# GpSimd makes the low part of every fourth weight chunk in the expert passes

## The chip, the cores and the metric

One core of a Trainium2 chip runs the whole kernel. The metric is the device time of one launch in microseconds. Three runs of the kernel before took 2875.26, 2880.69 and 2881.18 us; their median is 2880.69.

## The reference, cut to what matters

The reference is two transformer blocks over 512 tokens of width 1024 in float32. The part that the change touches is the `peer` layer of the first block: each token picks 16 of 16384 experts for each of 8 heads by product keys, and each expert is one row of `expert_u` and one of `expert_v`:

```python
cand = (s_top[:, :, 0, :, None] + s_top[:, :, 1, None, :]).reshape(T, PEER_HEADS, K * K)
...
# act = gelu(h . u_e) of the chosen experts, weighted by the softmax of the scores,
# output = sum over the chosen experts of weight * act * v_e
```

The kernel computes it in two ways. For 128 of the tokens it gathers the rows of the chosen experts. For the other 384 it multiplies with all experts, and masks out those that were not chosen.

## The kernel before

Matrix products are made exact to about float32 by splitting both operands into a high part (`wH`, rounded to fp32r) and a low part (`wL`, the rest), and adding three products: `three` (L380) issues low activations times high weights, high activations times low weights, and high times high.

Weights come in chunks of 128 x 2048 float32, 1 MB each, numbered through the whole kernel. Chunk k is loaded by the SP queue into `stage[k % 2]` (`load`, L330), ScalarE copies it to `wH[k % 4]` (`split_hi`, L342, line L347 in the profile), VectorE subtracts to get `wL[k % 4]` (`split_lo`, L349, line L352), and TensorE multiplies it (`chunk`, L1851, waits for the low part). There are two stage buffers, so the load of chunk k waits until the low part of chunk k - 2 is made; the SP queue works in order, so that a waiting load holds all that are queued behind it. The high part of chunk k waits until TensorE has begun chunk k - 3 (`w_begun`).

The expert passes are chunks 24 to 151 (`C_PEER` to `C_FFN1`): 64 of `u_l`, then 64 of `v_l`. In step s of the first pass TensorE multiplies chunk s of the pass, while the engines split the chunk two steps ahead. VectorE's other work in these passes, in its own order of instructions, is:

- Steps 0 to 19: the top-k selection, in four blocks of tokens `tt` (from L1386 on). Each block has four low parts in it: at its begin, after the indices (L1420), after the comparison of L1424 and after the weights. In block 1 the row addresses are made (`row_places`, L1368) right before the second of the four, that of chunk 7 of the pass. They release GpSimd's gathers. From block 2 on, each low part is followed by two or three row products (`row_dot`, L1352).
- Steps 20 to 43: the masks of the chosen experts (`hits`, L1455 to L1465), four in each step, with a low part after the second, and two or three row products. TensorE spreads them (L2124).
- Steps 44 to 63: a low part and two or three row products in each step. From step 62 on, the second pass's activations are begun as well.
- Second pass: in each step (`peer_dve`, L1489) a low part, two products of activation and gate (L1498), the low parts of the activations (L1503) after ScalarE's high parts (L849), and two row sums (`row_sum`, L1359; four in each of two early steps). TensorE waits for the low parts of the activations before each chunk. In SP's queue the load of a chunk stands behind the load of the gates (L514), and every second time also behind that of the masks (L520).

GpSimd issues 256 gathers of 128 rows of 4 KB (L1810), 128 of `u_rows` and then 128 of `v_rows`, into four row buffers. From the fifth on it waits before each until VectorE has used the row four before (`s_g["used"]`). Elsewhere it makes a few low parts of activations, 128 x 512 each (L1794, L1800, L1816).

## Time and profile before

| | |
|---|---|
| median of three runs | 2880.69 us |
| profiled execution | 2877.29 us |
| its span | 2875.5 us |
| TensorE busy | 2710.2 us (94%) |
| VectorE busy | 2206.8 us (77%) |
| ScalarE busy | 948.1 us (33%) |
| GpSimd busy | 387.3 us (13%) |
| chain that ended last | TensorE 74%, VectorE 16%, DMA 5% |
| the low parts of the weights, VectorE | 256, 536.9 us |

PE is TensorE's matmuls, PEld its weight loads, DVE VectorE, ACT ScalarE, POOL GpSimd, SPq the queue of SP. In a row of a timeline the first number is the start in us from the start of the span, the second the time from the start of the first to the end of the last instruction of the row, and "xN" how many instructions it holds. In brackets stand the idle time of the engine before it and what ended it. TensorE runs the first pass from about 548 to 1190 us, the second to about 1720 us.

### The profile page before, as it was taken

To read this page: it belongs to the slowest core of one execution; us is meant where nothing else is said; L and a number is where in the kernel's file an instruction comes from. 1 tells how busy PE (TensorE), PEld (TensorE's weight loads), DVE (VectorE), ACT (ScalarE), POOL (GpSimd) and SP (SyncE) were. 2 spreads that over 40 slices of the span, in tenths; PEclk is the share of its full clock that TensorE was granted. 3 is DMA by queue.
4 is the path that set the end of the run, shared out by engine and by line. 5 is a ranking of instruction groups with operands and counts; after the bars stand their busy time and mean duration, and the time that the engine had idled before them with its cause. 6 is when DMAs were issued, how large, how long until landed. Compare 5 with 4: busy or idle time off the path is not lost.

```text
span 2875.5 us, 39138 instructions
## 1 busy us (share of the span) xinstructions
PE 2710.2 (94%) x13863; PEld 2344.4 (82%) x13863; DVE 2206.8 (77%) x3758; ACT 948.1 (33%) x1238; POOL 387.3 (13%) x275
## 2 busy tenths in 40 slices
PE   7976999998999999999999997999999998999998
PEld 6752567898999999999999994788877874788886
DVE  6566748999899977688888877778786476578787
ACT  3211433333444433333333322222224255322222
POOL 0001000014222244243333330000000000000000
PEclk9986999999999999999999997999999998999999
DMA  6234012257788899999999980222222200122221
GB/s 254 77 133 152 34 33 88 98 200 251 274 305 296 299 352 365 326 357 347 346 348 348 348 323 37 74 94 102 88 103 86 90 30 1 53 106 97 88 102 66
DMA packets 159039, 515.58 MB, mean 179 GB/s; under 512 B 11745, under 2 KB 77665, under 8 KB 127329
## 3 DMA queue, kind: packets, MB, share of 16 engines
q1 hardware_dynamic: 109840, 326.62, 32.2%
q0 software_dynamic: 36864, 134.23, 12.7%
q10 hardware_dynamic: 12240, 53.48, 4.7%
q8 instruction: 57, 0.93, 0.1%
q14 instruction: 38, 0.30, 0.0%
HBM read 461.86 MB, written 52.43 MB: 179 GB/s over the span
## 4 chain that ended last, share of the span: by engine, by line
PE 74%; DVE 16%; DMA 5%; issue 2%; ACT 2%; POOL 0%; SPq 0%; ACTq 0%; DVEq 0%
PE ps L382 21%; PE ps L386 21%; PE ps L385 21%; PE ps L2124 3%; DVE sb_wL L352 3%; DMA sb_stage<-w_ada_l 2%; PE ps L2330 1%; PE ps L2340 1%; DVE sb_rows L1352 1%; DMA sb_stage<-v_l 1%; PE ps L2051 1%; DMA sb_stage<-u_l 1%; DMA sb_ada<-w_ada_l 1%; DVE sb_ada_sum L1211 1%; ACT sb_wH L347 1%
## 5 line engine op out<-in xcount | busy, mean ns | idle before, releaser
L382 PE MATMUL ps<-sb_hL,sb_wH 128*128 128x512 f32 (+1 forms) x2240 | 840.9, 375 | 25.5 <-DVE sb_wL L352 17.5
L386 PE MATMUL ps<-sb_hH,sb_wH 128*128 128x512 f32 (+1 forms) x2240 | 822.4, 367 | 0.0
L385 PE MATMUL ps<-sb_hH,sb_wL 128*128 128x512 f32 (+1 forms) x2240 | 821.4, 367 | 0.0
L352 DVE TENSOR_TENSOR sb_wL<-sb_stage,sb_wH 128x2048 fp32r<-128x2048 f32 (+2 forms) x256 | 536.9, 2099 | 207.9 <-ACT sb_wH L347 207.1
L347 ACT ACTIVATE sb_wH<-sb_stage 128x2048 fp32r<-128x2048 f32 (+2 forms) x256 | 445.4, 1757 | 319.8 <-PE ps L382 171.7
L382 PEld LDWEIGHTS ps<-sb_hL,sb_wH 128*128 128x128 f32 x2240 | 424.7, 190 | 84.6 <-DVE sb_wL L352 19.0
L385 PEld LDWEIGHTS ps<-sb_hH,sb_wL 128*128 128x128 f32 x2240 | 424.7, 190 | 54.6 <-issue 6.6
L386 PEld LDWEIGHTS ps<-sb_hH,sb_wH 128*128 128x128 f32 x2240 | 423.4, 189 | 50.1
L382 PE MATMUL ps<-sb_waL,sb_wH 128*128 128x384 f32 x1024 | 346.8, 339 | 8.2 <-DVE sb_waL L1503 8.2
L386 PE MATMUL ps<-sb_waH,sb_wH 128*128 128x384 f32 x1024 | 345.4, 337 | 0.0
L385 PE MATMUL ps<-sb_waH,sb_wL 128*128 128x384 f32 x1024 | 345.3, 337 | 0.0
L1810 POOL DMA_INDIRECT sb_rows<-u_rows,sb_row_at x128 | 177.6, 1388 | 711.0 <-DVE sb_rows L1352 375.4
L1810 POOL DMA_INDIRECT sb_rows<-v_rows,sb_row_at x128 | 189.8, 1482 | 353.5 <-DVE sb_tok L1359 317.4
L1623 DVE TENSOR_TENSOR sb_xT<-sb_xT,ps 128x512 f32<-128x512 f32 x304 | 198.4, 685 | 28.8 <-PE ps L386 27.3
L382 PEld LDWEIGHTS ps<-sb_waL,sb_wH 128*128 128x128 f32 x1024 | 193.4, 189 | 10.1 <-DVE sb_waL L1503 10.0
L385 PEld LDWEIGHTS ps<-sb_waH,sb_wL 128*128 128x128 f32 x1024 | 193.4, 189 | 0.0
L386 PEld LDWEIGHTS ps<-sb_waH,sb_wH 128*128 128x128 f32 x1024 | 193.2, 189 | 0.0
L891 ACT ACTIVATE sb_gel<-sb_gcv 128x512 f32<-128x512 f32 x44 | 27.8, 632 | 473.6 <-DVE sb_gcv L1650 473.6
L1359 DVE SCALAR_TENSOR_TENSOR sb_tok<-sb_rows,sb_row_act,sb_tok 128x1024 f32<-128x1024 f32 x128 | 164.1, 1282 | 14.4 <-DMA sb_rows<-v_rows,sb_row_at 5.9
L1352 DVE SCALAR_TENSOR_TENSOR sb_rows<-sb_rows,sb_tok 128x1024 f32<-128x1024 f32 x128 | 152.6, 1223 | 13.3 <-DMA sb_rows<-u_rows,sb_row_at 13.2
L792 ACT ACTIVATE sb_ga<-ps 128x384 f32<-128x384 f32 x128 | 62.1, 490 | 242.4 <-PE ps L386 240.1
L382 PE MATMUL ps<-sb_faL,sb_wH 128*128 128x512 f32 x336 | 133.3, 397 | 3.3 <-DVE sb_fa L1656 1.8
(358 smaller groups left out, 3346.4 us busy)
## 6 DMA issues: line engine op xcount, KB each, us to landing
sb_stage<-u_l SPq DMA_DIRECT2D x64, 1024.0 KB, 6.1
sb_stage<-v_l SPq DMA_DIRECT2D x64, 1024.0 KB, 7.9
sb_stage<-up_l SPq DMA_DIRECT2D x44, 1024.0 KB, 4.7
g_scratch<-sb_ga ACTq DMA_DIRECT2D x64, 384.0 KB, 6.2
w_scratch<-sb_wst ACTq DMA_DIRECT2D x12, 2048.0 KB, 9.1
sb_wg<-w_scratch SPq DMA_DIRECT2D x32, 768.0 KB, 6.3
sb_scr<-g_scratch SPq DMA_DIRECT2D x64, 384.0 KB, 4.5
sb_stage<-down_l SPq DMA_DIRECT2D x44, 512.0 KB, 3.2
```

Of the source, the lines that this page charges most:

```text
L347: act.activation(wH[k % SLOTS][:, 0:n], stage[k % STAGES][:, 0:n], ACT.Copy).then_inc(w_hi, 1)
L352: dve.tensor_tensor(wL[k % SLOTS][:, 0:n], stage[k % STAGES][:, 0:n], wH[k % SLOTS][:, 0:n], ALU.subtract).then_inc(w_split, 1)
L382: m = pe.matmul(dst, lh, rl, start=first, stop=False)
L385: pe.matmul(dst, ll, rh, start=False, stop=False)
L386: return pe.matmul(dst, lh, rh, start=False, stop=last)
L792: act.activation(ga[s0 % 2][:, m, :], ps[:, 2 * (s0 % 2) + m, 0:TD], ACT.Gelu).then_inc(s_u["gelu"], 1)
L1211: op = dve.scalar_tensor_tensor(total[:, :], w, sc[:, k:k + 1], total[:, :], ALU.mult, ALU.add)
L1352: dve.scalar_tensor_tensor(rows[r % 4][:, :], rows[r % 4][:, :], 1.0, tok[:, :], ALU.mult, ALU.mult, accum_out=column(row_act, r, i, per)) ...
L1359: dve.scalar_tensor_tensor(tok[:, :], rows[r % 4][:, :], column(row_act, r, i, per), tok[:, :], ALU.mult, ALU.add).then_inc(s_g["used"], 1)
L1623: dve.tensor_tensor(xT[:, d, :], xT[:, d, :], ps[:, 4 + d % 4, :], ALU.add).then_inc(s["added"], 1)
L1810: pool.indirect_dma_start(rows[r % 4][:, :], None, A["u_rows" if r < ROUNDS else "v_rows"], bass.IndirectOffsetOnAxis(ap=row_at[:, r % ROU ...
L2124: m = pe.matmul(ps[:, 4 + g0 % 4, q * P:(q + 1) * P], oneJ[g0 % 4][:, q, :], oneI[g0 % 4][:, q, :], start=True, stop=True)
```

## The change

Within the expert passes, the low part of every fourth chunk (the fourth, the eighth and so on, 32 in all) is made by GpSimd, with a semaphore `w_low` of its own; the other 96 stay on VectorE. `split_done` says which semaphore and which count stand for a chunk; the loads and TensorE wait for that. The operation, its operands and its size are the same. On GpSimd the first of them stands ahead of the first gather. The others stand between the gathers: that of the chunk which VectorE would split in step s comes before the first gather that would wait for a row used in step s, and after at least four gathers. `step_of_round` computes the step in which a row is used.

```diff
+        w_low = sem("w_low")
...
+        def step_of_round(r):
+
+            if r < ROUNDS_A:
+                return 8 + next(n for n in range(8) if r < ROUNDS_A * (n + 1) // 8)
+            r -= ROUNDS_A
...
+        def by_pool(k):
+
+            return C_PEER <= k < C_FFN1 and (k - C_PEER) % 4 == 3
+
+        def split_done(k, i=0, per=0):
+
+            assert per in (0, 4)
+            if by_pool(k):
+                return w_low, (k - C_PEER) // 4 + 1 + i * (per // 4)
+            before = max(0, min(k, C_FFN1) - C_PEER) // 4
+            return w_split, k + 1 - before + i * (per // 4 * 3 if C_PEER <= k < C_FFN1 else per)
+
+        def load(sp, k, src, i=0):
+
             n = src.shape[-1]
             if k >= STAGES:
-                sp.wait_ge(w_split, c - (STAGES - 1))
+                sp.wait_ge(*split_done(k - STAGES, i, 0 if isinstance(i, int) else 4))
...
         def split_lo(dve, k, n=CHUNK, i=0, per=0):
 
+            if by_pool(k):
+                return
             dve.wait_ge(w_hi, k + 1 + i * per)
...
+            def pool_split(k):
+
+                pool.wait_ge(w_hi, k + 1)
+                pool.tensor_tensor(wL[k % SLOTS][:, :], stage[k % STAGES][:, :], wH[k % SLOTS][:, :],
+                                   ALU.subtract).then_inc(w_low, 1)
+
+            splits = [k for k in range(C_PEER, C_FFN1) if by_pool(k)]
+            pool_split(splits.pop(0))
             pool.wait_ge(s_g["at"], 1)
             for r in range(2 * ROUNDS):
+                while splits and r >= 4 and splits[0] - C_PEER - 2 <= step_of_round(r - 4):
+                    pool_split(splits.pop(0))
                 if r >= 4:
                     pool.wait_ge(s_g["used"], r - 3)
                 pool.indirect_dma_start(rows[r % 4][:, :], None, A["u_rows" if r < ROUNDS else "v_rows"],
...
             def chunk(k, i=0, per=0):
-                pe.wait_ge(w_split, k + 1 + i * per)
+                pe.wait_ge(*split_done(k, i, per))
```

## Rows read from the trace of the kernel before

**Rows 1.** The page's costliest groups: line, engine, operation, count, busy, mean ns, idle before.
```profile
L382 PE MATMUL ps<-sb_hL,sb_wH 128*128 128x512 f32 (+1 forms) x2240 | 840.9, 375 | 25.5 <-DVE sb_wL L352 17.5
```

**Rows 2.** Windows: length, busy us of each engine, granted clock, DMA share, GB/s.
```profile
640.00:650.00 10.00, 5.10 (x16) 5.10 (x17) 9.97 (x10) 0.43 (x2) 3.44 (x2) 0.66 0.49 175
...
680.00:690.00 10.00, 1.67 (x10) 1.35 (x8) 9.69 (x31) 4.26 (x5) 0.00 (x0) 0.71 0.17 66
...
720.00:730.00 10.00, 8.81 (x51) 8.76 (x51) 3.38 (x2) 0.37 (x2) 0.00 (x0) 1.00 0.87 303
...
900.00:1000.00 100.00, 100.00 (x671) 100.00 (x670) 93.06 (x214) 43.12 (x58) 21.07 (x16) 1.00 0.80 294
...
1240.00:1250.00 10.00, 8.88 (x51) 8.55 (x50) 9.17 (x9) 2.86 (x3) 6.00 (x4) 1.00 1.00 349
...
1400.00:1500.00 100.00, 100.00 (x578) 99.81 (x577) 80.78 (x85) 34.29 (x36) 35.20 (x24) 1.00 0.95 346
```

**Rows 3.** GpSimd's subtractions (groups; ns min/median/max), and VectorE beside the second.
```profile
L1800 POOL TENSOR_TENSOR sb_hL<-sb_qk,sb_hH 128x512 fp32r<-128x512 f32 x4 | 5.1, 1263 | 277.3 <-ACT sb_hH L699 277.3
...
L1794 POOL TENSOR_TENSOR sb_qnL<-sb_lat,sb_qnH x2: 1437/1606/1775, 283.5 to 285.2; 128x512 fp32r<-128x512 f32 x2
...
283.47 0.69 DVE L1115 TENSOR_TENSOR sb_lat<-sb_lat,sb_scr 96x512 f32<-96x512 f32 x1
```

**Rows 4.** Timeline around chunks 7 to 10 of the first pass: start, length, what.
```profile
603.55 2.29 DVE L352 TENSOR_TENSOR sb_wL<-sb_stage,sb_wH 128x2048 fp32r<-128x2048 f32 x1
603.80 3.00 POOL L1810 DMA_INDIRECT sb_rows<-u_rows,sb_row_at  x1 [315.71 <-DVE sb_row_at L1373]
...
606.12 19.53 SPq L336 DMA_DIRECT2D sb_stage<-u_l  x4
...
610.16 2.29 DVE L352 TENSOR_TENSOR sb_wL<-sb_stage,sb_wH 128x2048 fp32r<-128x2048 f32 x1
611.36 1.90 POOL L1810 DMA_INDIRECT sb_rows<-u_rows,sb_row_at  x1 [0.30 <-issue]
...
622.82 2.29 DVE L352 TENSOR_TENSOR sb_wL<-sb_stage,sb_wH 128x2048 fp32r<-128x2048 f32 x1 [2.14 <-ACT sb_wH L347]
...
631.29 0.49 ACT L792 ACTIVATE sb_ga<-ps 128x384 f32<-128x384 f32 x1 [3.67 <-PE ps L386]
```

**Rows 5.** The same timeline: the low part of chunk 11.
```profile
642.55 2.29 DVE L352 TENSOR_TENSOR sb_wL<-sb_stage,sb_wH 128x2048 fp32r<-128x2048 f32 x1
```

**Rows 6.** The same timeline: high part of chunk 19, low parts of 18 and 19.
```profile
716.44 1.92 ACT L347 ACTIVATE sb_wH<-sb_stage 128x2048 fp32r<-128x2048 f32 x1 [3.06 <-DMA sb_stage<-u_l]
...
718.90 4.48 DVE L352 TENSOR_TENSOR sb_wL<-sb_stage,sb_wH 128x2048 fp32r<-128x2048 f32 x2
```

**Rows 7.** The same timeline: a row product of the mask stretch.
```profile
775.24 1.23 DVE L1352 SCALAR_TENSOR_TENSOR sb_rows<-sb_rows,sb_tok 128x1024 f32<-128x1024 f32 x1 [1.61 <-DMA sb_rows<-u_rows,sb_row_at]
```

**Rows 8.** The same timeline: begin of the second pass, chunks 71 and 72.
```profile
1235.51 2.28 DVE L352 TENSOR_TENSOR sb_wL<-sb_stage,sb_wH 128x2048 fp32r<-128x2048 f32 x1
1236.70 1.90 POOL L1810 DMA_INDIRECT sb_rows<-v_rows,sb_row_at  x1 [0.30 <-issue]
...
1239.87 5.44 DVE L1359 SCALAR_TENSOR_TENSOR sb_tok<-sb_rows,sb_row_act,sb_tok 128x1024 f32<-128x1024 f32 x4
...
1245.23 2.29 DVE L352 TENSOR_TENSOR sb_wL<-sb_stage,sb_wH 128x2048 fp32r<-128x2048 f32 x1
...
1248.65 1.03 DVE L1503 TENSOR_TENSOR sb_waL<-sb_scr,sb_waH 128x384 fp32r<-128x384 f32 x2 [0.20 <-ACT sb_waH L849]
```

**Rows 9.** The same timeline: one step in the middle of the second pass.
```profile
1402.86 0.94 POOL L1810 DMA_INDIRECT sb_rows<-v_rows,sb_row_at  x1 [0.30 <-issue]
...
1406.42 1.03 DVE L1503 TENSOR_TENSOR sb_waL<-sb_scr,sb_waH 128x384 fp32r<-128x384 f32 x2 [0.20 <-ACT sb_waH L849]
...
1407.37 2.70 DVE L1359 SCALAR_TENSOR_TENSOR sb_tok<-sb_rows,sb_row_act,sb_tok 128x1024 f32<-128x1024 f32 x2
...
1409.36 1.92 ACT L347 ACTIVATE sb_wH<-sb_stage 128x2048 fp32r<-128x2048 f32 x1 [2.56 <-PE ps L382]
```

More of the change, by code:

```diff
@@ L310, in build @@
         s_g = sems("rows", "tok", "copied", "at", "ld0", "ld1", "ld2", "ld3", "used", "gelu", "out")
+        def step_of_round(r):
+            if r < ROUNDS_A:
+                return 8 + next(n for n in range(8) if r < ROUNDS_A * (n + 1) // 8)
+            r -= ROUNDS_A
+            for n, begin, end, per in ((ROUNDS_B, W_FIRST, W_FIRST + 4, ROUNDS_B // 4),
+                                       (FIRST_C - ROUNDS_A - ROUNDS_B, W_FIRST + 4, W_END, ROUNDS_W // 4),
+                                       (ROUNDS - FIRST_C - ROUNDS_L, W_END, PEER_STEPS - 4, ROUNDS_C // 4),
+                                       (ROUNDS_L, PEER_STEPS - 4, PEER_STEPS, ROUNDS_L // 4)):
+                if r < n:
+                    return begin + r // per
+                r -= n
+            if r < FIRST_SUMS[4]:
+                return PEER_STEPS + 2 + next(q for q in range(4) if r < FIRST_SUMS[q + 1])
+            return PEER_STEPS + min(6 + (r - FIRST_SUMS[4]) // (ROUNDS_V // 4), PEER_STEPS - 2)
         def row_landed(r, i=0, per=0):
@@ L327, in build @@
         stored = sem("stored")
-        def load(sp, c, src, c0=None):
-            k = c if c0 is None else c0
+        def by_pool(k):
[7 more added lines that the diff above has]
+        def load(sp, k, src, i=0):
             n = src.shape[-1]
             if k >= STAGES:
-                sp.wait_ge(w_split, c - (STAGES - 1))
+                sp.wait_ge(*split_done(k - STAGES, i, 0 if isinstance(i, int) else 4))
             sp.dma_start(stage[k % STAGES][:, 0:n], src).then_inc(ld_stage[k % STAGES], 16)
@@ L496, in _ @@
                 for q in range(4):
-                    load(sp, C_PEER + 2 + q + 4 * i, A["u_l"][4 * i + q + 2], C_PEER + 2 + q)
+                    load(sp, C_PEER + 2 + q, A["u_l"][4 * i + q + 2], i)
             for s in range(PEER_STEPS - 2, PEER_STEPS):
@@ L537, in _ @@
                 for q in range(4):
-                    load(sp, C_V + 3 + q + 4 * i, A["v_l"][4 * i + q + 3], C_V + 3 + q)
+                    load(sp, C_V + 3 + q, A["v_l"][4 * i + q + 3], i)
                     gate_load(2 + q, i)
@@ L554, in ffn_loads @@
                     for q in range(2):
-                        load(sp, c + 3 + 2 * q + 4 * i, A["up_l"][l, 2 * i + q + 2], c + 3 + 2 * q)
-                        load(sp, c + 4 + 2 * q + 4 * i, A["down_l"][l, 2 * i + q + 1], c + 4 + 2 * q)
+                        load(sp, c + 3 + 2 * q, A["up_l"][l, 2 * i + q + 2], i)
+                        load(sp, c + 4 + 2 * q, A["down_l"][l, 2 * i + q + 1], i)
                 load(sp, c + 2 * FT - 5, A["up_l"][l, FT - 2])
@@ L1812, in _ @@
                                         ).then_inc(s_g[f"ld{r % 4}"], 16)
+            for k in splits:
+                pool_split(k)
             for h in range(DIFF_H):
```

## The prediction, made before the change ran

> **What bounds the kernel now.** I read first the page's list of costliest groups, for what TensorE waits on. In the whole span its largest matmul group sat idle 25.5 us in front of its instructions, 17.5 us of it for VectorE's low parts [rows 1]. Then the windows: TensorE is busy for all of 900 to 1000 and of 1400 to 1500 at full granted clock, with VectorE at 93.1 and 80.8 of 100 us [rows 2]. There nothing taken off VectorE can help. The gaps are in the top-k stretch (5.10 of 10 us busy at 640, clock 0.66; 1.67 at 680; 8.81 at 720) and at the start of the second pass (8.88 at 1240) [rows 2]. I number the expert chunks e = k - 24, so 0 to 63 belong to the first pass and 64 to 127 to the second; GpSimd gets 3, 7, 11 and so on, 32 in all.
>
> **What a moved low part costs.** On VectorE it takes 2.29 us [rows 4]. On GpSimd this form does not occur. Nearest is the same subtraction on 512 columns, 1.263 us [rows 3]. Four times that is 5.05 us, the upper bound. VectorE goes from 0.69 us at 512 columns [rows 3] (96 partitions there) to 2.29 at 2048, a factor of 3.3, which on GpSimd would be 4.2 us, the lower bound. I take 4.6, between them. 
> **The two engines block each other.** One of GpSimd's low parts took 1.775 us instead of 1.263: it began at 283.51, while VectorE ran an operation with two SBUF inputs until 284.16 [rows 3]. The gathers show it too: the one at 603.80 ends at 606.80, 0.96 us after VectorE's subtraction of 603.55 is over, and the one at 611.36 ends 0.8 us after the subtraction begun at 610.16 [rows 4]. So GpSimd waits until such a VectorE operation is over. I take it to hold the other way round too: while GpSimd subtracts, VectorE's operations with two SBUF inputs (low parts, row products, row sums, masks) wait up to 4.6 us. No row shows this direction, so its price lies between 0 and 5.05 us each; I take the full one. The Trainium skill (SBUF — State Buffer, Who interferes with whom) states it: a VectorE instruction with two SBUF inputs and a GpSimd instruction that reads SBUF exclude each other, and the second to issue waits for the first to finish. By that rule the forecast stands; a kernel in which it did not hold is rival 1.
>
> **Top-k stretch, chunks 3 to 19: -6.6 us, then +6.9, then +4.3.** VectorE paces TensorE here, and each load waits for the split two chunks before, on one queue in order. Chunk 3: its low part leaves VectorE, whose work moves 2.3 us forward. Chunk 7: VectorE made it at 603.55, right after the row addresses [rows 4]. GpSimd must first issue four gathers, which took from 603.80 to 613.26 [rows 4]. With the addresses at 601.2 and the same waits behind VectorE's two pairs of 2.2 us operations and chunk 8's low part, the fourth gather ends at about 610.9, the split waits for the last operation (612.3) and ends at 616.9. The load of chunk 9 was issued at 606.12 [rows 4] and now waits until 616.9; the load of chunk 10 queues behind it. The former took 5.4 us to its high part (611.55). So chunk 9 has its high part at 624.4 and its low part at 626.7, and TensorE, which ended this chunk at 631.29 [rows 4] and so began it at 623.0, waits some 3.7 us. Chunk 10's low part starts at about 627.5 instead of 622.82 [rows 4]: VectorE enters the third block of tokens 4.7 us late, having been about 2.2 early: a detour of 6.9 us, in which the 2.2 us of chunk 7 itself are lost too. Chunks 11 and 15: GpSimd splits them some 10 us earlier than VectorE (642.55 [rows 5]), beside the top-8 searches, which read one input each, so without a clash. That removes the waits at 640 and 680 themselves, but the next chunks, 12 and 16, are paced by VectorE, and what TensorE keeps is 2 x 2.2 us. Before chunk 18 the balance is 4.7 - 4.4 = +0.3 us. Chunks 18 and 19: the high part of 19 ends at 718.36, VectorE starts the low part of 18 at 718.90, and TensorE is waiting for it [rows 2, 6]. Both shift alike, so GpSimd is ready 0.5 us before VectorE, and chunk 18 waits for GpSimd: 4.6 less 0.3 (semaphore, start) gives +4.3. Together **+4.6 us**. Bounds: -6.6 (three low parts off, and neither detour) and +6.
>
> **Mask stretch, 740 to 1000: +1 us.** Skipping a low part gives 2.3 us and the block costs 4.6 per four steps; VectorE has 7 us in 100 free [rows 2], some 3.3 us per four steps of 11.9. Only the first four steps have three row products and no slack; there the row waited for at 775.24 [rows 7] is gathered up to 1.8 us later. I take +1, bounds -0.5 and +3. From 1000 to 1180 a split of 4.6 us comes between gathers; the low part is done over a chunk ahead of TensorE, so 0, up to +2.
>
> **Start of the second pass: +2.3 us.** Chunk 71: its low part stood at 1235.51; GpSimd's fourth gather was at 1236.70 [rows 8]. Now the split begins there, at about 1238.1, and ends at 1242.7. The four row sums (5.44 us, 1239.87 [rows 8]) come behind it and end at 1248.1. Chunk 72's low part starts then instead of at 1245.23, and the low activations of that step, ready 4.45 us after its start (1249.68 [rows 8]), are ready at 1252.6. TensorE waited for them already, so it starts 2.9 us later; 0.6 us of its next wait disappears. Bounds: -1.5 (no block, the old wait goes) and +4, the load of chunk 69, queued behind chunk 67's split, among it.
>
> **Rest of the second pass, 14 splits: +0.4 us.** A chunk is 48 of the 578 matmuls in 100 us [rows 2], 8.3 us. Counted from a ScalarE high part, which starts with TensorE's chunk (1409.36 [rows 9], so the one before at 1401.05), the second gather ended at 2.8, the low activations at 6.4 and the row sums started at 6.3 [rows 9]. In a GpSimd step VectorE waits for no high part: low activations at 3.4, GpSimd from 3.4 to 8.0, row sums until 10.7, next low part 0.5 us late, and its activations at 15.2 against a need at 16.6. The next load goes out at 8.1 instead of 6.8, but the gate and spread loads in front of it go out 3.4 us earlier, so the transfers have the same end. Covered; if GpSimd wins against the second low activation, 0.3 us is lost. Bounds 0 and +7 (0.5 us each). Without the cover, 32 x 2.3 us (4.6 less 2.29) would be 74 us. Waits and semaphores: 32 more, beside other work.
>
> **Sum.** 4.6 + 1 + 2.3 + 0.4 = +8.3 us. Against the profiled execution (2877.29 us, 1.8 of it outside the span) that is 2885.6; against the median of the runs shown, 2880.69, it is 2889.0. The median lies 3.4 above the profiled run, so I start a little above the latter, at 2878.2, and name **2886.5 us**.
>
> **Rivals**, each from 2878.2.
> 1. No mutual block: VectorE runs freely beside GpSimd's subtraction. Then chunk 18 isn't held, the balance of the top-k stretch is about -1 (split 7 still stands behind four gathers), the mask stretch gives 0.5 and chunk 71 gives back 1.5: -3, **2875**, not slower. For it: no row shows VectorE waiting. Against it: the reverse is plain [rows 3, 4]. It decides at whether row sums and low parts next to a split last up to 7 us or their old 1.35 and 2.29.
> 2. VectorE is first at chunk 18. The race is 0.5 us and hangs on the landing of one load. 0.3 + 1 + 2.3 + 0.4 = +4.0, **2882**.
> 3. Chunk 9 comes in time: four gathers are issued faster and its load, on an idle DMA, lands before TensorE and VectorE need it. Then VectorE's lead is kept but for the 2.14 us that it waited at 622.82 [rows 4]: -2.1 - 4.4 + 4.3 + 3.7 = +1.5, **2880**. It decides at whether the low part of chunk 10 starts before 622.8. Against it: the load would have to go out some 6 us sooner than worked out. With rival 1 besides it would be -2.1 - 4.4 - 0.5 - 1.5 = -8.5, **2870**: there all the time taken off VectorE reaches TensorE.
> 4. The 14 steps of the second pass each lose 0.7 us, because the load goes out behind the split while DMA is busy 95% of the time [rows 2], and lands after its high part is due: +10 more, **2896**.
>
> **How the numbers follow.** Forecast (block, GpSimd first at 18) 0.42; rival 1 0.13; rival 2 0.18; rival 3 0.07 and 0.05 with rival 1; rival 4 0.15. The range, 2874 to 2897, leaves out rivals 1 and 3 together, the lower part of rival 1 and what lies beyond rival 4. Under 0.2% (5.8 us) can't be told from no change in this kernel. Around the median, faster is below 2875: rivals 1 and 3 together and half of rival 1, 0.12. Slower is above 2886.4: about two thirds of the forecast (its terms are rather bounds than not) and rival 4, 0.45. Within: 0.43.
>
> **What the profile would show.** Right: GpSimd's subtractions of 4.2 to 5.05 us, longer where VectorE was first; VectorE's two-input operations of 4 to 7 us beside them; a TensorE wait at about 623 that wasn't there; no wait at 11 and 15 but at 12 and 16; the low part of 18 held; a wait of some 4 us at about 1250; none from 1300 to 1700. Wrong: VectorE's durations unchanged (rival 1), chunk 10's low part before 622.8 (rival 3), or TensorE short of full in 1400 to 1500 (rival 4).

## The result, and the profile after

The changed kernel takes **2929.14 us**, median of four runs (2922.91 to 2938.6), beside 2880.93 for the kernel before in the same session: ratio 1.0176, 95% interval 1.0158 to 1.0195, 48 us slower. (The ratios here are those on record and need not be the quotient of the medians, which is 1.0167 here.) The forecast was 2886.5, with 2897 as the upper end. The sign was right and the size was not: 48 us instead of 8.

The profiled execution of after spans 2936.5 us (2875.5 before). The lines that answer to [rows 1] and [rows 3], from the page's and the trace's groups; the last two are new groups that matter now:

```profile
L412 PE MATMUL ps<-sb_hL,sb_wH 128*128 128x512 f32 (+1 forms) x2240 | 843.6, 377 | 38.1 <-DVE sb_wL L382 15.9
...
L1839 POOL TENSOR_TENSOR sb_wL<-sb_stage,sb_wH 128x2048 fp32r<-128x2048 f32 x32 | 148.9, 4652 | 286.2 <-ACT sb_wH L375 285.8
...
L1533 DVE TENSOR_TENSOR sb_waL<-sb_scr,sb_waH 128x384 fp32r<-128x384 f32 x128 | 136.8, 1109 | 27.8 <-ACT sb_waH L879 27.5
L1495 DVE TENSOR_SCALAR sb_scr<-sb_tab,sb_fromsel 128x128 f32<-128x128 f32 x384 | 132.6, 409 | 0.0
```

The same two groups before, which the forecast had no rows for:

```profile
L1465 DVE TENSOR_SCALAR sb_scr<-sb_tab,sb_fromsel 128x128 f32<-128x128 f32 x384 | 106.9, 345 | 0.0
L1503 DVE TENSOR_TENSOR sb_waL<-sb_scr,sb_waH 128x384 fp32r<-128x384 f32 x128 | 65.8, 556 | 14.9 <-ACT sb_waH L849 14.6
```

VectorE gave up 32 low parts of 2.29 us, 73 us, and got back 71 us in the low activations (136.8 - 65.8) and 26 us in the tensor_scalars of the masks alone (132.6 - 106.9): it stands and waits inside them.

Windows of after (columns as in [rows 2]):

```profile
640.00:650.00 10.00, 10.00 (x60) 10.00 (x59) 9.72 (x29) 5.67 (x6) 1.82 (x1) 1.00 0.44 146
680.00:690.00 10.00, 10.00 (x59) 10.00 (x58) 9.66 (x70) 2.57 (x3) 4.66 (x2) 1.00 0.89 338
720.00:730.00 10.00, 4.74 (x23) 4.46 (x23) 8.21 (x2) 2.48 (x4) 4.53 (x1) 0.90 0.55 189
900.00:1000.00 100.00, 94.97 (x627) 94.59 (x627) 90.03 (x192) 41.98 (x56) 30.08 (x18) 0.98 0.75 276
...
1400.00:1500.00 100.00, 99.75 (x566) 98.92 (x565) 85.91 (x80) 32.78 (x36) 49.21 (x27) 1.00 0.97 339
```

The gaps at 640 and 680 are gone from these windows, as forecast, and the one at 720 is longer. The second of them has only moved by one chunk: TensorE now stands still for 9.8 us up to 704.2, ahead of chunk 16, where before it stood 9.7 us ahead of chunk 15. What was not forecast stands in the fourth line: 5 us of every 100 are lost in the mask stretch, where TensorE had been busy all the time.

**Where the 61 us of the span went.** I cut the trace by the starts of TensorE's chunks: the start of the first of the 16 low-activation matmuls of each chunk in the trace's list of matmuls. The table holds the differences of such starts, in us, for both kernels and for the experiments below; "end" is the last matmul of the second pass (at 1738.6 us in before, not at about 1720). Each row is one profiled execution. That of after is the slowest of its four runs, 9.5 us above their median, and that of before lies 3.6 below its median, so the two profiles are 61 us apart where the medians are 48.

| kernel | chunks 0-20, top-k | 20-46, masks | 46-66 | 66-end |
|---|---|---|---|---|
| before | 190.4 | 304.1 | 171.5 | 525.0 |
| after | 200.6 | 327.7 | 188.2 | 538.3 |
| p1, splits 3 to 19 | 200.3 | 302.7 | 172.4 | 533.4 |
| p2, 23 to 43 | 191.2 | 327.0 | 172.0 | 534.7 |
| p3, 47 to 63 | 190.8 | 302.9 | 185.0 | 526.0 |
| p4, 67 to 127 | 190.4 | 304.9 | 172.6 | 538.2 |
| p5, zeros for all 32 | 195.5 | 318.4 | 185.9 | 522.2 |
| p6, masks, half splits | 191.1 | 307.8 | 172.7 | 525.7 |
| p7, masks, in pieces | 191.3 | 312.0 | 171.6 | 526.5 |
| p8, 3, 7 early, 11, 15 | 185.8 | 302.9 | 172.7 | 533.4 |
| p9, as p3, earlier | 192.0 | 302.9 | 185.1 | 533.7 |
| p10, ten in top-k | 198.9 | 302.9 | 172.0 | 525.8 |
| p11, ten, in pieces | 205.4 | 303.1 | 170.7 | 532.7 |
| p12, all 32 in pieces | 197.7 | 311.1 | 184.2 | 538.7 |
| p13, as p3, 64 columns | 191.6 | 305.2 | 175.6 | 524.6 |
| p14, as p3, half | 190.8 | 303.4 | 172.0 | 524.7 |
| p15, as p8 and 6 | 185.1 | 302.7 | 176.6 | 534.5 |

After against before: +10.2, **+23.6**, **+16.7** and +13.3 us, 63.8 in all (2.8 of it is regained outside). The last column has a spread of its own that the change does not make: without splits in it, it is either 524 to 527 or 532 to 535 (see the last section), so of the 13.3 up to 8 may be that. In the third column kernels without splits there lie between 170.7 and 176.6, and all of that spread is in its last chunk. From the start of chunk 46 to that of chunk 65 before, the kernels without a split there, p13 and p14 all take 158.1 to 158.3 us; after takes 171.6, p3 168.5, p5 168.7, p9 166.6 and p12 167.8. Chunk 65 itself takes 12.6 to 18.3 us in the kernels that lose nothing up to there, 16.7 in after.

What it looks like at each place, in the timeline of after. Top-k (answers to [rows 4] and [rows 6]), the third line being TensorE's first matmul of chunk 7:

```profile
600.73 3.00 POOL L1850 DMA_INDIRECT sb_rows<-u_rows,sb_row_at  x1 [38.56 <-DVE sb_row_at L1403]
...
610.21 5.73 POOL L1839 TENSOR_TENSOR sb_wL<-sb_stage,sb_wH 128x2048 fp32r<-128x2048 f32 x1
615.99 0.69 PE L412 MATMUL ps<-sb_hL,sb_wH 128*128 128x384 f32 x1 [11.52 <-POOL sb_wL L1839]
...
628.83 2.29 DVE L382 TENSOR_TENSOR sb_wL<-sb_stage,sb_wH 128x2048 fp32r<-128x2048 f32 x1 [2.90 <-ACT sb_wH L375]
...
721.53 4.53 POOL L1839 TENSOR_TENSOR sb_wL<-sb_stage,sb_wH 128x2048 fp32r<-128x2048 f32 x1 [2.06 <-ACT sb_wH L375]
721.63 6.57 DVE L382 TENSOR_TENSOR sb_wL<-sb_stage,sb_wH 128x2048 fp32r<-128x2048 f32 x1
```

The mask stretch, the end of the first pass, and (answering to [rows 8] and [rows 9]) the second pass. Each pair is one VectorE line and the GpSimd split that it meets:

```profile
760.89 6.04 DVE L1495 TENSOR_SCALAR sb_scr<-sb_tab,sb_fromsel 128x128 f32<-128x128 f32 x4
761.81 4.52 POOL L1839 TENSOR_TENSOR sb_wL<-sb_stage,sb_wH 128x2048 fp32r<-128x2048 f32 x1
...
1147.09 6.19 DVE L1382 SCALAR_TENSOR_TENSOR sb_rows<-sb_rows,sb_tok 128x1024 f32<-128x1024 f32 x1 [0.67 <-DMA sb_rows<-u_rows,sb_row_at]
1147.65 4.53 POOL L1839 TENSOR_TENSOR sb_wL<-sb_stage,sb_wH 128x2048 fp32r<-128x2048 f32 x1
...
1286.38 5.93 DVE L1533 TENSOR_TENSOR sb_waL<-sb_scr,sb_waH 128x384 fp32r<-128x384 f32 x2 [0.20 <-ACT sb_waH L879]
1287.31 4.57 POOL L1839 TENSOR_TENSOR sb_wL<-sb_stage,sb_wH 128x2048 fp32r<-128x2048 f32 x1
...
1424.79 5.71 DVE L1533 TENSOR_TENSOR sb_waL<-sb_scr,sb_waH 128x384 fp32r<-128x384 f32 x2 [0.96 <-ACT sb_waH L879]
1424.98 4.63 POOL L1839 TENSOR_TENSOR sb_wL<-sb_stage,sb_wH 128x2048 fp32r<-128x2048 f32 x1
```

Four tensor_scalars take 1.1 us when nothing is beside them, a row product 1.22, two low activations 1.03. Each has grown by 4.7 to 5 us.

### The profile page after: what moved, and what is told of

It reads as the page before. It is cut to its first block, busy times and chain, and to the rows that moved or that the text cites. A ratio compares the mean times of both kernels' runs of the same rounds, so it can differ in the third digit from the quotient of the medians.

```text
span 2936.5 us, 39113 instructions
## 1 busy us (share of the span) xinstructions
PE 2731.4 (93%) x13863; PEld 2362.3 (80%) x13863; DVE 2259.8 (77%) x3726; ACT 946.3 (32%) x1238; POOL 562.5 (19%) x307
## 4 chain that ended last, share of the span: by engine, by line
PE 70%; DVE 13%; issue 6%; DMA 6%; ACT 3%; POOL 2%; SPq 0%; DVEq 0%; ACTq 0%
PE ps L412 20%; PE ps L416 20%; PE ps L415 19%; PE ps L2166 2%; DMA sb_rows<-u_rows,sb_row_at 2%; DMA sb_stage<-w_ada_l 2%; DVE sb_wL L382 1%; DMA sb_stage<-v_l 1%; DVE sb_rows L1382 1%; PE ps L2372 1%; ACT sb_wH L375 1%; PE ps L2382 1%; POOL sb_rows L1850 1%; DVE sb_scr L1495 1%; PE ps L2093 1%
## 5 line engine op out<-in xcount | busy, mean ns | idle before, releaser
L382 DVE TENSOR_TENSOR sb_wL<-sb_stage,sb_wH 128x2048 fp32r<-128x2048 f32 (+1 forms) x224 | 467.7, 2090 | 163.0 <-ACT sb_wH L375 162.5
L1850 POOL DMA_INDIRECT sb_rows<-u_rows,sb_row_at x128 | 194.9, 1523 | 391.4 <-DVE sb_rows L1382 331.7
L1850 POOL DMA_INDIRECT sb_rows<-v_rows,sb_row_at x128 | 198.8, 1553 | 276.4 <-DVE sb_tok L1389 242.4
L1382 DVE SCALAR_TENSOR_TENSOR sb_rows<-sb_rows,sb_tok 128x1024 f32<-128x1024 f32 x128 | 169.5, 1357 | 54.9 <-DMA sb_rows<-u_rows,sb_row_at 53.6
L1839 POOL TENSOR_TENSOR sb_wL<-sb_stage,sb_wH 128x2048 fp32r<-128x2048 f32 x32 | 148.9, 4652 | 286.2 <-ACT sb_wH L375 285.8
L1533 DVE TENSOR_TENSOR sb_waL<-sb_scr,sb_waH 128x384 fp32r<-128x384 f32 x128 | 136.8, 1109 | 27.8 <-ACT sb_waH L879 27.5
```

The source lines that it names most:

```text
L382: dve.tensor_tensor(wL[k % SLOTS][:, 0:n], stage[k % STAGES][:, 0:n], wH[k % SLOTS][:, 0:n], ALU.subtract).then_inc(w_split, 1)
L1382: dve.scalar_tensor_tensor(rows[r % 4][:, :], rows[r % 4][:, :], 1.0, tok[:, :], ALU.mult, ALU.mult, accum_out=column(row_act, r, i, per)) ...
L1533: dve.tensor_tensor(waL[s0 % 2][m][:, :], wa[m], waH[s0 % 2][m][:, :], ALU.subtract).then_inc(s_e["lo"], 1)
L1839: pool.tensor_tensor(wL[k % SLOTS][:, :], stage[k % STAGES][:, :], wH[k % SLOTS][:, :], ALU.subtract).then_inc(w_low, 1)
L1850: pool.indirect_dma_start(rows[r % 4][:, :], None, A["u_rows" if r < ROUNDS else "v_rows"], bass.IndirectOffsetOnAxis(ap=row_at[:, r % ROU ...
```

## Experiments: which splits cost how much

All kernels are made from the changed one. The set of chunks that GpSimd splits is a list in them, the two counters follow from it, and SyncE's loop over the first pass is cut where the set changes; this moves the line numbers by some six (the split is L1845, the low parts L387, the masks' tensor_scalars L1501).

```
def by_pool(k):
    return k - C_PEER in POOLED      # p1: range(3, 20, 4)   p2: range(23, 44, 4)
                                     # p3: range(47, 64, 4)  p4: range(67, 128, 4)
```

> GpSimd makes the low parts of chunks 3, 7, 11, 15 and 19 alone (top-k stretch); all others stay on VectorE. Theory (the loss is a sum of local losses, each where a split stands): the profiled change lags 8.5 us behind before when TensorE begins chunk 21, so this kernel is slower than before by 7 to 10 us, about 2889. The chunk starts 7 and 18 are late as in the full change. Rival (what is lost in the top-k stretch is made up later, because the later stretches have slack): within 3 us of before, about 2882.

> GpSimd makes the low parts of chunks 23, 27, 31, 35, 39 and 43 alone (mask stretch). Theory (local losses: VectorE's tensor_scalars of the masks and its subtractions are held for one split each, and TensorE has no slack there): +20 to +25 us, about 2903, four us for each of the six splits. Rival (the prediction's +1 is right by itself, and the stretch only loses when VectorE comes into it late from the top-k stretch): +1 to +5, about 2884.

> GpSimd makes the low parts of chunks 47, 51, 55, 59 and 63 alone (end of the first pass). Theory (local losses: splits queued behind gathers that wait for rows used): the full change lost 3.3 and 2.8 at chunks 54 and 55, 0.6 at 58 and 59, 4.2 at 63, and part of 2.6 and 3.3 at 64 and 65: +8 to +15 us, about 2892. Rival (these waits come from rows that are late already because of the mask stretch): within 3 us of before, about 2882.

> GpSimd makes the low parts of chunks 67, 71 and so on to 127 alone (second pass). Theory (local losses): 3 to 5 at the start of the pass and 0.4 to 0.9 for each of the 14 later splits, +12 to +18 us, about 2896. If all four parts are independent, their losses add up to 48 us. Rival (as predicted: the steady second pass is covered): +2.7 us, about 2884, and the four parts do not add up to 48.

Measured against before: p1 2887.95 us, ratio 1.0025 (1.0009 to 1.0041); p2 2903.2, 1.0079 (1.0055 to 1.0102); p3 2887.56, 1.0018 (1.0001 to 1.0035); p4 2888.28, 1.0029 (1.0018 to 1.0040). The four excesses add up to 1.51%, 43.5 us, of the full change's 1.76%; the difference lies within their intervals. p1 and p2 came out as expected. p3 and p4 are slower, but by less than expected: their ratios say 5 and 8 us (p3's interval reaches from 0.3 to 10), where +8 to +15 and +12 to +18 were expected, and more than the rivals gave. In the table the four kernels have +9.9, +22.9, +13.5 and +13.2 in their own columns, beside +10.2, +23.6, +16.7 and +13.3 in after, and next to nothing in the others, apart from the 8 us in the last column of p1 and p2, which is that column's own spread. **The losses are local**, and within the noise they add up; the rival that the mask stretch only loses because VectorE comes into it late is out, since p2 comes into it in time and loses the same.

## Experiments: what holds VectorE

p5 keeps every queue, semaphore and gather, and GpSimd only writes:

```
-                pool.tensor_tensor(wL[k % SLOTS][:, :], stage[k % STAGES][:, :], wH[k % SLOTS][:, :],
-                                   ALU.subtract).then_inc(w_low, 1)
+                pool.memset(wL[k % SLOTS][:, 0:1024].bitcast(mybir.dt.uint8), 0)
+                pool.memset(wL[k % SLOTS][:, 1024:2048].bitcast(mybir.dt.uint16), 0).then_inc(w_low, 1)
```

> The full change with one replacement: instead of subtracting, GpSimd fills the same low parts with zeros, in two fills chosen to last about as long together (4 to 6 us); the low parts of every fourth chunk are thus left out. Queue order, semaphores and gathers stay. It tells what holds VectorE. Theory A: GpSimd's reading is what excludes VectorE's two-input operations, and the masks' tensor_scalars are held for another reason, their own use of both ports (the Trainium skill, SBUF - State Buffer, Who interferes with whom, says both). Then the low activations of the second pass are back at a mean of 0.56 us (1.11 in the change) and the low part of chunk 18 at 2.29, while the tensor_scalars stay at a mean above 0.40 (0.345 before); the mask stretch still costs some 20 us, the rest less: about 2910. Rival B: all is held by reads alone: both are back, 2885 to 2892. Rival C: any long GpSimd operation holds VectorE, or the loss comes from queue order: as the full change, 2925 to 2935.

Measured 2906.73, ratio 1.0090 (1.0068 to 1.0112), near the 2910 of theory A and with its groups:

```profile
L1845 POOL MEMSET sb_wL<- 128x4096 uint8 x32 | 113.1, 3535 | 284.6 <-ACT sb_wH L380 284.6
L1846 POOL MEMSET sb_wL<- 128x2048 uint16 x32 | 58.8, 1837 | 0.0
...
L1501 DVE TENSOR_SCALAR sb_scr<-sb_tab,sb_fromsel 128x128 f32<-128x128 f32 x384 | 131.8, 478 | 0.0
L1539 DVE TENSOR_TENSOR sb_waL<-sb_scr,sb_waH 128x384 fp32r<-128x384 f32 x128 | 65.8, 556 | 25.1 <-ACT sb_waH L885 24.6
```

and, at the low part of chunk 18, with a fill of 3.51 us beside it:

```profile
722.78 3.51 POOL L1845 MEMSET sb_wL<- 128x4096 uint8 x1 [2.02 <-ACT sb_wH L380]
722.91 2.28 DVE L387 TENSOR_TENSOR sb_wL<-sb_stage,sb_wH 128x2048 fp32r<-128x2048 f32 x1
```

The low activations are back at 556 ns and the low part of 18 at 2.28 us (6.57 in after), and no row product or row sum beside a fill takes longer than 1.29 us: operations with two SBUF inputs are held by GpSimd's reads and not by its writes. (One mask product takes 1.65 us instead of 0.69, at 813.93; it stands right behind a tensor_scalar that is held until the same moment.) The tensor_scalars are held still: 478 ns, and 131.8 us of busy time, as in after (the means count overlapping time twice, so between these two kernels the busy time is the one to compare). So there are **two holds**, and removing one left the other. The Trainium skill (SBUF — State Buffer, Who interferes with whom) states both: an operation with two SBUF inputs contends with a GpSimd instruction that reads SBUF, not with one that only writes, and a tensor_scalar can run in a mode that takes both port pairs. The trace agrees with the first, with the numbers above, and with what follows for the second; that the tensor_scalars are in that mode no run here shows. In the table, p5 loses 0 in the second pass and 5.1 of 10.2 in the top-k stretch, 14.3 of 23.6 in the masks, and still 14.4 of 16.7 in chunks 46 to 66, where the cause must be another one.

p6 shortens GpSimd's instruction, p7 cuts it up:

```
p6:  pool.tensor_tensor(wL[k % SLOTS][:, 0:1024], stage[k % STAGES][:, 0:1024], wH[k % SLOTS][:, 0:1024], ...
p7:  for c in range(0, CHUNK, 512):
         op = pool.tensor_tensor(wL[k % SLOTS][:, c:c + 512], stage[k % STAGES][:, c:c + 512], ...
```

> As the kernel with the six splits of the mask stretch (2903, +21), but GpSimd subtracts only the first 1024 of 2048 columns of each; the other half is left out. Theory (VectorE is held for the length of GpSimd's instruction, and TensorE's wait is that length less the lead of the masks): TensorE waited 3.0 to 3.4 us per split of 4.5, so the lead is 1.3; with 2.3 us it waits 1.0 and the granted clock drops for less: 6 x 1.0 to 1.5 less the 2.2 gained ahead of the first mask, so +4 to +7, about 2888. Rival (the loss comes from the late gathers or from the queues, or is proportional to the length): +10 and more, 2893 or later.

> As the kernel with the six splits of the mask stretch (2903, +21), but GpSimd subtracts each in four instructions of 512 columns. Theory: each instruction of about 1.26 us excludes VectorE anew and VectorE gets one operation in between two of them; VectorE then does four operations in the same 4.5 to 5 us in which it did none: its loss falls by some 1.1 us per split, 2893 to 2900. Rival A: VectorE gets nothing in between (the four count as one): 2903. Rival B: the two-way exclusion makes both slower, each waiting for the other in turn: 2905 and more.

Measured: p6 2883.26, ratio 1.0011 (0.9996 to 1.0027); p7 2887.33, 1.0033 (1.0012 to 1.0054). TensorE's waits from 740 to 1100 (in all, times, longest), in p2, p6 and p7:

```profile
PE ps L2173 <- DVE sb_scr L1501: 16.5, 6, 3.4
...
PE ps L2173 <- DVE sb_scr L1501: 3.4, 6, 1.2
...
PE ps L2175 <- DVE sb_scr L1501: 6.2, 6, 3.8
```

Half the length leaves a fifth of the wait: 16.5 / 6 = 2.8 us per split of 4.5, and 0.6 per split of 2.4. The masks are thus some 1.8 us ahead of TensorE, and what of a hold is longer is TensorE's. The trace of before has nearly this lead in it: of the six groups of four tensor_scalars that p2's splits hold, the last ends 1.1 to 1.6 us before TensorE starts with the group. p5 fits as well: its longest single hold there is the first fill, 3.5 us, and each of its last four splits cost TensorE's chunk 1.6 to 1.7. p6's loss, 3.7 us in the table, is a little less than the 4 to 7 expected, and far from its rival's 10. On top comes the clock, which I had given no term. In p2, TensorE stood still for 3.03 us until 808.80, and from there to 812.2 its granted clock is 0.50 (the 1.2 GHz level); the matmuls in it are slow.

```profile
808.80 2.08 PE L2173 MATMUL ps<-sb_scr 128*128 128x128 f32 x8 [3.03 <-DVE sb_scr L1501]
...
811.31 0.52 PE L421 MATMUL ps<-sb_hH,sb_wH 128*128 128x384 f32 x1
...
812.24 0.34 PE L421 MATMUL ps<-sb_hH,sb_wH 128*128 128x384 f32 x1
```

That chunk lost 4.87 us, 3.03 of it by the wait. In p2 four of the six splits cost TensorE's chunk 4.3 to 5.2 us and two 2.8, the wait alone. The granted clock fell to the lower level for 3.4 us at just those four. The wait's length doesn't tell them apart: 3.37, 3.03, 2.52 and 2.52 us with the fall, 2.53 and 2.52 without. p7 came out better than I expected: from the third split on each cost about 0.5 instead of 2.8 to 4.3 (the first 5.4, the second 1.7). The tensor_scalars slip in between the pieces: those begun at 803.77 and 805.00 take 1.3 us each and end with a piece. p12 shows that not everything does.

> The full change (32 low parts at its places), each in four instructions of 512 columns. Theory: what the holds cost shrinks (mask stretch +5.7 instead of +21 as measured alone, low part of 18 and the steady second pass about nothing), what the queue order costs stays (chunks 7 and 9, and 54 to 66): together about +25, 2905. Rival (the queue-order losses grow, because a split in pieces lasts longer and gathers come later): 2915 or more.

Measured 2916.71, ratio 1.0131 (1.0109 to 1.0154): the rival's figure, but not its mechanism, since the losses of the queue order didn't grow (top-k 197.7 beside 200.6 in after, third column 184.2 beside 188.2). The masks gained as in p7 (311.1), the last column nothing (538.7). Its low activations average 1115 ns, as in after, and two of its places tell why:

```profile
728.57 7.08 POOL L1846 TENSOR_TENSOR sb_wL<-sb_stage,sb_wH 128x512 fp32r<-128x512 f32 x4 [1.75 <-ACT sb_wH L380]
728.99 3.03 DVE L387 TENSOR_TENSOR sb_wL<-sb_stage,sb_wH 128x2048 fp32r<-128x2048 f32 x1
...
1441.23 6.17 DVE L1539 TENSOR_TENSOR sb_waL<-sb_scr,sb_waH 128x384 fp32r<-128x384 f32 x2 [0.88 <-ACT sb_waH L885]
1441.48 5.03 POOL L1846 TENSOR_TENSOR sb_wL<-sb_stage,sb_wH 128x512 fp32r<-128x512 f32 x4
```

The low part of 18 was let in after the first piece (3.03 us, and GpSimd's four grew to 7.08). The low activations, which began 0.25 us before the first piece, waited out all four. So my expectation that pieces cure every hold was wrong; when a two-input operation gets in between is open.

## Experiments: chunks 46 to 66

Neither hold explains this part, since p5 keeps the loss. I took the place in GpSimd's queue for the cause: in p3 the high part of chunk 59 began at 1137.61 and lasted 1.92, but its split began at 1147.94, behind gathers that waited for rows used. p9 puts each split one step earlier:

```
-                while splits and r >= 4 and splits[0] - C_PEER - 2 <= step_of_round(r - 4):
+                while splits and r >= 4 and splits[0] - C_PEER - 3 <= step_of_round(r - 4):
```

> As the kernel with the splits of chunks 47, 51, 55, 59 and 63 alone (2887.6; from chunk 46 to chunk 66 it took 185.0 us where before took 171.5), but each split stands one step, three rounds of gathers, earlier in GpSimd's queue. Theory (the loss is queue order: the high part of 59 was there at 1139.5 and its split began at 1147.9, behind gathers that wait for rows used): TensorE no longer waits for chunks 59 and 63, and 46 to 66 takes 172 to 177 us. Rival A (the hold of VectorE's row products by the splits, 5.5 and 6.2 us long, makes the rows late, and that is the loss): 46 to 66 stays at 182 or more. Rival B: the split now waits for its high part and holds the gathers up: 185 or more.

Measured 2894.87, ratio 1.0064 (1.0044 to 1.0084), and 185.1 us: my theory fell. By the finer cut, up to the start of chunk 65, p9 loses 8.5 us where p3 loses 10.4, so 2 us came back at most. The splits did start sooner, 1.5 to 3.7 us after their high parts instead of up to 8.4, but TensorE's waits went over to VectorE's low parts. The figures of both rivals came out. A can't be the whole cause, since in p5 no row product is held (the longest beside a fill takes 1.23 us) and the loss is there. B's wait is in the trace once: the split of chunk 47 waited 10.65 us for its high part, with the gathers behind it, but no chunk before 53 lost by it; the later splits waited for nothing. TensorE's waits for low parts from 1060 to 1260 in p3 and in p9:

```profile
PE ps L417 <- POOL sb_wL L1845: 3.6, 1, 3.6
...
PE ps L417 <- DVE sb_wL L387: 4.3, 3, 3.1
```

What all have in common is 4.6 us or more of GpSimd's own time. p13 and p14 shorten that and change nothing else:

```
p13: pool.tensor_tensor(wL[k % SLOTS][:, 0:64], stage[k % STAGES][:, 0:64], wH[k % SLOTS][:, 0:64], ...
p14: pool.tensor_tensor(wL[k % SLOTS][:, 0:1024], stage[k % STAGES][:, 0:1024], wH[k % SLOTS][:, 0:1024], ...
```

> As the kernel with the splits of chunks 47, 51, 55, 59 and 63 alone, at their places in the queue, but GpSimd subtracts only the first 64 of 2048 columns of each; the rest of these low parts is left out. Chunks 46 to 66 took 171.5 us before and 185.0 with whole splits; the fill with zeros (no hold of row products) and the earlier place in the queue left it at 185.9 and 185.1. Theory R (GpSimd's own time: the rows go round in four buffers, product, gather, landing, and 4.6 us in which GpSimd gathers nothing make the rows late, whether or not VectorE is held): with a split of a few tenths of a us it is gone, 46 to 66 takes 171 to 174 us. Rival Q (the place behind gathers makes the low part of 59 and the load of 61 late, at any length of the split): the split of 59 still begins some 8 us after its high part and 46 to 66 stays at 177 or more.

> The same with the first 1024 of 2048 columns (2.4 us); the other half of these low parts is left out. Theory R: the loss falls faster than the length, as the ring of rows has some slack: 46 to 66 takes 172 to 178 us. Rival Q: 180 or more, nearly as with whole splits.

Measured: p13 2883.31, ratio 1.0012 (1.0001 to 1.0024), 175.6 us; p14 2877.61, 0.9992 (0.9980 to 1.0004), 172.0 us. VectorE's waits for gathered rows from 1060 to 1200 in before, p3, p5, p14 and p15:

```profile
DVE sb_rows L1352 <- DMA sb_rows<-u_rows,sb_row_at: 7.3, 15, 1.0
...
DVE sb_rows L1388 <- DMA sb_rows<-u_rows,sb_row_at: 39.1, 19, 5.3
...
DVE sb_rows L1388 <- DMA sb_rows<-u_rows,sb_row_at: 60.5, 22, 9.2
...
DVE sb_rows L1388 <- DMA sb_rows<-u_rows,sb_row_at: 23.5, 21, 5.3
...
DVE sb_rows L1388 <- DMA sb_rows<-u_rows,sb_row_at: 35.1, 14, 3.3
```

With 2.4 us in place of 4.7, at the same place in the queue, the loss is gone (172.0 against 171.5), so rival Q is out. The third column of p13 missed its bound by 1.6 us, but by the finer cut p13 and p14 take 158.1 us up to chunk 65, as before does: nothing is lost with either. The splits' lateness goes with it: that of chunk 59 starts 8.4 us after its high part in p3, 0.9 in p13 and 0.1 in p14. **The length of GpSimd's own work is what counts**, with 4.6 us in one instruction or 5.4 in p5's two fills, whether or not VectorE is held, and not the place in the queue by itself. By the runs alone, without the profiles, this is weaker: p3's and p14's intervals just overlap (1.0001 to 1.0035, 0.9980 to 1.0004), and p13 can't be told from p3.

How the length becomes TensorE's wait is in part argued. Rows go round in four buffers (product, gather, landing), two or three rounds per chunk of 8.3 us, and GpSimd gathers nothing while it splits. VectorE waits longer for rows (39.1 and 60.5 us), GpSimd's next splits stand behind gathers that wait for rows used, and so start late; VectorE's low parts stand behind the late rows. But late rows alone cost nothing: p15 has no split in this stretch, waits 35.1 us for rows there and loses nothing up to chunk 65. Between 2.4 and 4.6 us some slack is used up; that it is the ring's is not shown, and a ring of more buffers was not tried.

## Experiments: the top-k stretch, and a faster version

p8 leaves out chunk 19 and puts the split of 7 ahead of the wait for the row addresses:

```
+            while splits and splits[0] - C_PEER <= 7:
+                pool_split(splits.pop(0))
             pool.wait_ge(s_g["at"], 1)
```

> GpSimd makes the low parts of chunks 3, 7, 11 and 15 alone, and that of chunk 7 stands in its queue ahead of the wait for the row addresses, so ahead of the first four gathers. Theory (the detour at chunk 7 came from the four gathers ahead of the split): no wait at chunks 7 and 9, the four moved low parts give back up to 2.2 us each where VectorE paces TensorE: 5 to 9 us faster than before, about 2875. Rival (the block gives as much back: GpSimd's splits meet VectorE's two-input operations of the selection, or the loads in order take the gain): within 2 us of before.

Measured **2876.3, ratio 0.9973 (0.9958 to 0.9987)**, faster than both kernels (5 us below before by the medians), with 185.8 us to chunk 20, 4.6 less than before and 14.5 less than p1. All four splits lie beside the top-8 searches, whose operations take 0.22 to 0.3 us there as elsewhere; only that of chunk 7 reaches past them and holds a copy for 2.5 us. How much of the 14.5 us is due to the place of chunk 7 and how much to leaving out 19 was not run apart. p15 adds chunk 6:

> GpSimd makes the low parts of chunks 3, 6, 7, 11 and 15 alone, those of 3, 6 and 7 ahead of the wait for the row addresses. Chunk 6 is added to the four that gave 0.27% because its high part is ready just as VectorE goes over to the searches, which read one input, so the split meets none of VectorE's two-input operations. Theory (the chain of VectorE's selections sets the end of the stretch, and only splits beside the searches are free): chunk 20 begins 183 to 184.5 us after chunk 0 (185.8 with four, 190.4 before) and the time is 0.3 to 0.45% under before. Rival (VectorE then waits 2.3 us longer for the high part of 10): 185.8, as with four.

Measured 2875.3, 0.9982 (0.9972 to 0.9993), 185.1 us to chunk 20: between the two expectations, and the time is 0.18% under before, less than the 0.3 to 0.45% expected. Its split of chunk 7 stands later than in p8, beside a tensor_scalar, which takes 4.58 us instead of 0.23. One more low part was worth 0.7 us there, and the times of p8 and p15 can't be told apart.

If four pay, do ten?

```
-                while splits and r >= 4 and splits[0] - C_PEER - 2 <= step_of_round(r - 4):
+                while splits and {3: 0, 7: 0, 11: 6, 12: 6, 13: 6, 15: 11, 16: 16, 17: 16, 18: 16, 19: 19}[splits[0] - C_PEER] <= r:
```

The dictionary says ahead of which gather each chunk's split stands.

> GpSimd makes ten low parts of the top-k stretch: 3, 7, 11, 12, 13, 15, 16, 17, 18 and 19, each placed in its queue where its high part is due (3 and 7 ahead of the addresses, 11 to 13 ahead of the seventh gather, 15 ahead of the twelfth, 16 to 18 ahead of the seventeenth, 19 ahead of the twentieth). Theory (VectorE's selections pace this stretch, each low part taken off it is worth up to 2.3 us, and a split costs VectorE only where it meets two-input operations or tensor_scalars): VectorE is done 5 to 9 us sooner than with four of them (chunk 20 began 185.8 us after chunk 0): chunk 20 begins 175 to 182 us after chunk 0, and the time is about 2870. Rival (the holds give back what is taken off, GpSimd is full): chunk 20 at 186 or more after chunk 0, and 2876 or more.

> The ten low parts as in the run before this one, each in four instructions of 512 columns. Theory (a hold lasts for one instruction, so short ones cost VectorE less): one to four us faster than with whole ones. Rival (GpSimd's queue is the limit here and four instructions take longer than one, 5.4 against 4.65 us): as fast or slower than with whole ones.

Measured: p10 2886.23, ratio 1.0030 (1.0015 to 1.0046), 198.9 us; p11 2889.96, 1.0044 (1.0029 to 1.0059), 205.4 us. Both theories fell. TensorE's waits from 540 to 740 in p8, and to 760 in p10; then the last two sums of the selection in before, p8 and p10, and what held them up in p10:

```profile
PE ps L417 <- DVE sb_wL L387: 13.6, 2, 9.8
...
PE ps L2166 <- DVE sb_chosen L1477: 27.7, 2, 18.4
...
714.51 4.47 DVE L1385 TENSOR_REDUCE sb_chosen<-sb_scr 128x128 f32<-128x2048 f32 x2
...
707.41 4.47 DVE L1421 TENSOR_REDUCE sb_chosen<-sb_scr 128x128 f32<-128x2048 f32 x2
...
723.06 4.47 DVE L1421 TENSOR_REDUCE sb_chosen<-sb_scr 128x128 f32<-128x2048 f32 x2
...
697.36 5.03 POOL L1845 TENSOR_TENSOR sb_wL<-sb_stage,sb_wH 128x2048 fp32r<-128x2048 f32 x1 [1.64 <-ACT sb_wH L380]
697.88 8.86 DVE L1460 TENSOR_TENSOR sb_scr<-sb_tab,sb_posf 128x2048 f32<-128x2048 f32 x2
```

In p10 TensorE waits for no low part any more. It waits for VectorE's gates, which it transposes ahead of chunks 13 and 17: a second wait of the same engine stood right behind the first. VectorE's selection ends 15.7 us later than in p8 (its last sums start at 723.06 against 707.41), 12.7 of it counted from chunk 0. Five splits of p10 hold an operation with two inputs: a row product of 1.22 us takes 5.6 to 5.7 three times, the weights' product 3.91 instead of 0.29, and the two comparisons of 4.49 take 8.86. That is 21 us held, against 14 us for the six low parts taken off VectorE; where the rest of the 12.7 comes from I can't say. In this stretch the splits that cost nothing lay beside the top-8 searches and beside the sums of the selection, which read one input (two splits of p10, begun at 637.69 and 685.56).

## Why the prediction was right and wrong

**Right.** A split costs 4.652 us on GpSimd (4.6 taken, bounds 4.2 and 5.05). The figure of the Trainium skill (GPSIMD Engine Reference, Elementwise), 4497 ns, is 0.16 below this mean; the shortest of the 32 took 4.52 and the median is 4.63. The block is mutual, in the direction that no row had shown, and at its full price: rival 1 is out. GpSimd was first at chunk 18, by 0.1 us: the low part took 6.57 us and chunks 16 and 17, up to the start of 18, took 4.3 us more (24.1 against 19.8; +4.3 forecast), so rival 2 is out. The wait at 640 went, and the one at 680 stands ahead of chunk 16 instead, as forecast. Chunk 10's low part began at 628.83 (about 627.5 forecast, 622.82 before), so rival 3 is out as well.

**Mask stretch, +1 forecast, +23.6 measured.** This is the step that failed. It set 2.3 us saved and 3.3 free per four steps against one hold of 4.6. The sum is right as an average and says nothing of a wait: the hold comes in one piece, and what counts is how far the masks are ahead of TensorE at that moment, 1.1 to 1.8 us. The rest, 2.8 us per split, is lost each time and no later slack brings it back. The prediction also had the masks among the operations with two SBUF inputs; those held are tensor_scalars with one, and p5 shows that GpSimd's writes hold them too. [Rows 2] showed VectorE busy for 93.1 us of 100 with TensorE busy for all of them; how far ahead it worked had to be read from the timeline, and I did not look. The lower clock after four of the six waits came on top.

**Chunks 46 to 66, 0 to +2 forecast, +16.7 measured.** The step reads "the low part is done over a chunk ahead of TensorE, so 0". I followed the split's own result at its old time and not the gathers around it. 13.5 of the 16.7 us are lost up to chunk 65. With 4.6 us per split GpSimd falls behind: its split of chunk 55 ends at 1152.2, and TensorE has stood still for 3.1 us for it. p14 shows that half of the time would have been free. By which way the rest of the loss reaches TensorE stays open.

**Top-k stretch, +4.6 forecast, +10.2 measured.** The four gathers ahead of the split of 7 were seen, and its end, 616.9 forecast, was 615.94. The step then followed the load of chunk 9 and left out TensorE itself, which wanted chunk 7 at 604.5: 11.5 us of wait for the line above it. About 8 us of that replaced waits further on (chunks 10 and 11 took 16.8 instead of 24.8). At the start of chunk 16 TensorE was 4.4 us behind where +0.3 was forecast; the held low part of 18 then cost the 4.3 forecast; and chunk 18 itself, which began after a wait of 5.3 us with a granted clock of 0.50 for 3.2 us, took 1.5 more, for which there was no term. The sum of the step came out 5.6 too low.

**Start of the second pass and its steady part, +2.3 and +0.4 forecast, +13.3 measured in the profile and +8.4 us by p4's runs.** The 14 splits were taken as covered; the note beside it, that GpSimd might win against the second low activation, was priced at 0.3 us in one place. It won nearly each time (1109 ns mean, twice 556). The hold forecast for chunk 71 fell on the low activations and not on the row sums. TensorE's waits from 1250 to 1750 grew from 3.3 to 14.7 us. p5, without that hold, has none of the loss (522.2). Between the starts of chunks 73 and 124, with 12 splits and TensorE's two paces (last section) mixed in it, after lost 7.7 us against 0.4 forecast for 14. Rival 4 named 14 x 0.7 us for this part and was nearest in size, by another cause: the load goes out late in its story, the low activation is held in the trace.

## What to carry to other kernels

Don't set a stall of another engine against average slack: set its length against the lead of the work that it holds, at its place, and follow what queues behind it on both engines. A helper engine's time is a resource where it also feeds a ring of buffers; halving its instruction can make it free, while moving it in its queue may not. Move work only to where the other engine runs operations that the helper's reads and writes don't hold, and stop there: four low parts beside the searches gave 0.27%, ten in the same stretch lost 0.30%.

## What the runs showed of the hardware that I had not expected

- Tensor_scalars with one SBUF tensor (128 columns, f32) wait for a GpSimd subtraction and for a GpSimd fill that only writes (409 and 478 ns mean, 345 before; 133 and 132 us busy, 107 before), while two-input operations pass beside a fill (2.28 us beside 3.51).
- The operation with the earlier start doesn't always win: the row product of 1147.09 began 0.56 us before the split and took 6.19 us, and the split took its plain 4.53. The Trainium skill's section named above lets the first to issue keep the ports; if so, the start in the trace isn't that moment.
- TensorE has two paces in the second pass that the granted clock (1.00 in both) doesn't tell: 579 and 568 matmuls in 1500 to 1600, 8.32 and 8.48 us a chunk, 7.6 us over 48 chunks. Before, p3, p5 to p7, p10, p13 and p14 had the one, p1, p2, p8, p9, p11 and p15 the other, and in after, p4 and p12 it changed back and forth after short waits. What selects it is open. A comparison of two profiles in this pass is worth no more than that.

```profile
1500.00:1600.00 100.00, 100.00 (x579) 100.00 (x578) 81.01 (x85) 34.29 (x36) 34.77 (x24) 1.00 0.96 345
...
1500.00:1600.00 100.00, 100.00 (x568) 100.00 (x567) 79.22 (x84) 34.30 (x36) 34.12 (x24) 1.00 0.94 338
```

The first line is of before, the second of p8.
